# Attention of a hybrid decoder block: where the first tiles' transpositions and products stand among the blocks of scores

## The reference, cut to what matters

```python
def block(args):                       # 128 queries at a time, all heads
    scores = (einsum('bqhd,bkhd->bhqk', qn_b, k_nope)
              + einsum('bqhd,bkd->bhqk', qr_b, k_rope)) * scale
    scores = where(mask, scores, -inf)  # causal
    p = softmax(scores, axis=-1)
    return einsum('bhqk,bkhd->bqhd', p, v)
```

## Time and profile before

| | |
|---|---|
| median of 3 runs | 2707.79 us (2706.94 to 2709.8) |
| the profiled execution: its own time | 2709.62 us |
| the profiled execution: span from first to last instruction | 2707.7 us |
| TensorE busy | 2587.3 us, 96% |
| VectorE busy | 1756.2 us, 65% |
| ScalarE busy | 850.6 us, 31% |
| GpSimd busy | 638.9 us, 24% |
| mean granted TensorE clock | 0.981 of full |
| attention phase, from the first scores to the last product | 1357 to 2160 us |

### The profile page before, as it was taken

One profiled execution on the slowest core, in us unless ns is written; L12 is line 12 of the kernel. 1 busy time (PEld: TensorE's weight loads), 2 busy tenths in 40 slices (PEclk: granted clock), 3 DMA queues, 4 the chain that ended last, 5 costly groups with the idle time before them and its releaser, 6 DMA issues. The chain is left out here.

```text
span 2707.7 us, 32612 instructions
## 1 busy us (share of the span) xinstructions
PE 2587.3 (96%) x12186; PEld 2128.1 (79%) x12186; DVE 1756.2 (65%) x2073; ACT 850.6 (31%) x1683; POOL 638.9 (24%) x592
## 2 busy tenths in 40 slices
PE   4989999999999999997899999999999889999998
PEld 4767888888888888786777887887887778888887
DVE  5787967979879779564367767767767522223442
ACT  3432111111111111232255555555555430201221
POOL 2132111111111111131033233233233220323422
PEclk8999999999999999998899999999999999999999
DMA  8053312212112121377812112112111074666542
GB/s 297 8 175 105 94 32 78 67 58 78 47 55 83 42 78 59 121 263 251 252 63 102 62 65 101 62 65 101 62 65 65 32 240 156 201 216 212 188 151 78
DMA packets 200848, 306.73 MB, mean 113 GB/s; under 512 B 18249, under 2 KB 119693, under 8 KB 190636
## 3 DMA queue, kind: packets, MB, share of 16 engines
q1 hardware_dynamic: 194620, 284.89, 32.1%
q0 software_dynamic: 6128, 20.45, 2.4%
HBM read 202.01 MB, written 103.28 MB: 113 GB/s over the span
## 5 line engine op out<-in xcount | busy, mean ns | idle before, releaser
L52 PE MATMUL ps_proj<-h_hi,w_hi 128*128 128x512 f32 x1696 | 669.5, 395 | 9.6 <-DVE h_lo L697 6.8
L54 PE MATMUL ps_proj<-h_hi,w_lo 128*128 128x512 f32 x1696 | 662.6, 391 | 0.0
L53 PE MATMUL ps_proj<-h_lo,w_hi 128*128 128x512 f32 x1696 | 662.4, 391 | 0.0
L812 DVE SCALAR_TENSOR_TENSOR acc<-u,taps_t,acc 128x2048 f32<-128x2048 f32 x240 | 629.0, 2621 | 8.5
L52 PEld LDWEIGHTS ps_proj<-h_hi,w_hi 128*128 128x128 f32 x1696 | 320.1, 189 | 79.0 <-issue 7.8
L53 PEld LDWEIGHTS ps_proj<-h_lo,w_hi 128*128 128x128 f32 x1696 | 320.1, 189 | 67.5 <-issue 2.2
L54 PEld LDWEIGHTS ps_proj<-h_hi,w_lo 128*128 128x128 f32 x1696 | 319.7, 189 | 67.1
L586 POOL TENSOR_TENSOR w_lo<-raw,w_hi 128x1024 fp32r<-128x1024 f32 x53 | 168.7, 3184 | 807.1 <-ACT w_hi L411 807.0
L1692 POOL TENSOR_SCALAR prob<-prob,rinv 128x512 f32<-128x512 f32 (+2 forms) x320 | 196.3, 630 | 355.3 <-DVE rinv L1646 355.1
L1651 DVE TENSOR_TENSOR pt_lo<-ps_t,pt_hi 128x512 fp32r<-128x512 f32 (+1 forms) x320 | 194.3, 610 | 98.3 <-ACT pt_hi L1574 94.2
L1574 ACT ACTIVATE pt_hi<-ps_t 128x512 fp32r<-128x512 f32 (+1 forms) x320 | 169.4, 531 | 240.7 <-PE ps_t L1486 240.6
(11 more groups left out here) (216 smaller groups left out, 4040.8 us busy)
## 6 DMA issues: line engine op xcount, KB each, us to landing
qlat<-qlat_dram SPq DMA_DIRECT2D x32, 1024.0 KB, 6.1
raw<-in_w_in_dram SPq DMA_DIRECT2D x52, 512.0 KB, 6.4
under_h<-in_w_ada_dram SPq DMA_DIRECT2D x8, 1024.0 KB, 11.2
ga_dram<-lat SPq DMA_DIRECT2D x8, 1024.0 KB, 5.0
gb_dram<-lat SPq DMA_DIRECT2D x8, 1024.0 KB, 5.0
agate_dram<-lat SPq DMA_DIRECT2D x8, 1024.0 KB, 5.0
conv_dram<-acc SPq DMA_DIRECT2D x8, 1024.0 KB, 3.9
bgate_dram<-lat SPq DMA_DIRECT2D x8, 1024.0 KB, 5.0
```

What stands on the lines that cost most here:

```text
L52: pe.matmul(out, wh, xh, start=first, stop=False)
L53: pe.matmul(out, wh, xl, start=False, stop=False)
L54: return pe.matmul(out, wl, xh, start=False, stop=last)
L812: dve.scalar_tensor_tensor(acc[:], u[:, n:n + S], tap(n), acc[:], ALU.mult, ALU.add).then_inc(conv_tap if n < TAPS - 1 else conv_done, 1)
```

## The change

In group 3 the tiles that stand with blocks 5, 6 and 7 now stand behind the first chunk of the block's scores, no longer behind the block. The event `S` of such a block is split into `SA` (first chunk) and `SB` (the other three, and the maximum over the chunks). The event `E` is split as well: `E` is now the exponentials alone, and `R` the reciprocal and the scaling, which stays behind the block's scores. Tile 3 moves from block 7 to block 8 (`share`). The diff:

```diff
@@ attention_phase
     LAG = 2
+    PART = {"S": slice(None), "SA": slice(0, 1), "SB": slice(1, None)}
     SLOTS = 3
@@ plan
-        share = {3: [0, 1, 1, 2], 1: [0, 2, 7, 7], 2: [0, 2, 3, 3]}
+        share = {3: [0, 1, 1, 1], 1: [1, 2, 7, 7], 2: [0, 2, 3, 3]}
         for s, (g, b) in enumerate(BLOCKS):
-            ev.append(("S", s))
+            split = g == NC_ - 1 and b > 0
+            ev.append(("SA" if split else "S", s))
             if s:
                 ev.append(("E", s - 1))
+            if split:
+                tiles(share[g][b])
+                ev.append(("SB", s))
+            if s:
+                ev.append(("R", s - 1))
             if s == 5:
                 ev.append(("W", 0))
             if s in (6, 7):
                 ev.append(("VS", s - 4))
-            if g in share:
+            if g in share and not split:
                 tiles(share[g][b])
-        ev.append(("E", len(BLOCKS) - 1))
+        ev += [("E", len(BLOCKS) - 1), ("R", len(BLOCKS) - 1)]
@@ TensorE
-                def scores(at, s):
+                def scores(at, s, chunks):
...
-                    for c in range(g + 1):
+                    for c in range(g + 1)[chunks]:
...
-                        elif e[0] == "S":
-                            scores(at, e[1])
+                        elif e[0] in PART:
+                            scores(at, e[1], PART[e[0]])
@@ VectorE
-                        elif kind == "S":
+                        elif kind in PART:
                             g, b = BLOCKS[n]
-                            for c in range(g + 1):
+                            for c in range(g + 1)[PART[kind]]:
...
-                            if g:
+                            if g and kind != "SA":
                                 n_max = chunk_no[n, g] + 1 - QB
...
-                        elif kind == "E":
+                        elif kind == "R":
```

## The result

The changed kernel took 2712.4 us (median of 20 runs, 2709.4 to 2718.5), the kernel before 2707.8 us (20 runs): a ratio of 1.0019, interval 1.0013 to 1.0025. So it is slower, by some 5 us (3.5 to 6.8). The direction and the range were right; the forecast of 9.5 us was too high by about a factor of two.

The account below looks back on a forecast made before the run. TensorE, busy 96% of the span, was taken as the bound, with tile 4 following block 7's maximum; 16.92 - 15.73 = 1.19 us, times 8 heads = 9.5 us, on 2707.8 gave 2717.3 us, range 2711.5 to 2721.

Parts of the forecast that it names:

- Tile 4 moves with block 7's maximum: End of block 7: a fixed chain of 5.19 us from its maximum to tile 4, whatever TensorE does in between.
- VectorE's chain of low part, maxima and exponentials: Blocks 4 to 7: maxima queued behind the waiting low part follow the previous exponentials; 1.19 us more per head, chance 0.82.
- T0's gate: Before block 5's second chunk: T0 waits for GpSimd's scaling of block 3, costing 0.5 to 0.8 us of TensorE's time.
- the three transitions: Block 4 to 5, 5 to 6 and 6 to 7: 5.58, 5.70 and 5.64 us, together 16.92 against 15.73 before.
- A wait of about 1 us in front of block 6's second chunk: A sign expected in the trace if right: TensorE waits about 1 us before block 6's second chunk.
- The sign in front of S8's second chunk: A sign expected in the trace if right: a wait of about 0.8 us before the second chunk of block 8's scores.
- The second rival, T0's gate alone: Block 5's second chunk starts late, at 2.2 to 2.5 us; 0.2 to 0.5 us per head, 2709.6 to 2712 us; chance 0.08.
- The first rival, filled waits are won: Blocks 5 to 7: TensorE sets the pace, ring waits are filled; 0.37 us less per head, 2704.8 us; chance 0.06.
- block 5's ring wait of 0.43 us: Between block 5's first and second chunk: 1.67 us where 1.24 would do, so about 0.43 us lost that a transposition could fill.
- a cover of 0.5 us at block 5: Block 5's second chunk is ready at 3.96 us at the latest, VectorE comes to its maximum at 4.42.
- The clock: Blocks 5 to 8: nothing added; as a rival, new waits lower the clock once in each head, 2751 us; chance 0.04.

Follow-up runs that it names:

- e1: The changed kernel with VectorE's low parts of tiles 0 to 2 put back behind the block's maxima and reciprocal; 1.0016 against the kernel before.
- e2: The kernel before with only tile 3 moved from block 7 to block 8; one run, 2707.0 us.
- e5: The changed kernel with block 3's reciprocal and scaling moved between block 4's second and third chunks, so T0 need not wait; 1.0019 against the kernel before.
- e6: The changed kernel with e1's low parts behind the maxima and e5's earlier scaling of block 3 together; 0.9996 against the kernel before.
- e3: The changed kernel with both splits of the values moved behind block 7's exponentials and scaling; 0.9986 against the kernel before.
- e4: The kernel before with both splits of the values moved behind block 7's exponentials and scaling; 0.9984 against the kernel before.
- e8: e6 with the splits of the values behind block 7's exponentials and scaling, and block 7 unsplit with tiles 2 and 3 behind it; 0.9972 against the kernel before.

## Why the prediction was right, and where it was off

*Tile 4 moves with block 7's maximum.* Right. The distance was 5.18 to 5.21 us in before, changed, e1, e2, e5 and e6, whatever TensorE had in between, and it fell only when the split of the values was taken out of GpSimd's list (e3, e4).

*VectorE's chain of low part, maxima and exponentials sets the interval.* Right as the mechanism of the changed kernel for blocks 5 and 6: e5 shows that T0's gate, worth 0.5 us of TensorE's time, is covered by it, as the prediction had it. At block 7 it no longer holds in full. There the prediction had more cover than at block 5, and the trace has none (rows from two narrow windows, the x2 row holding the second and third held maximum):

```profile
1483.14 1.43 DVE L1635 TENSOR_REDUCE nmax<-ps_ring 128x1 f32<-128x512 f32 x2
...
1483.62 0.23 PE L1481 MATMUL ps_ring<-mask,ident 128*128 128x128 bf16 x1
...
1483.88 0.69 DVE L1635 TENSOR_REDUCE nmax<-ps_ring 128x1 f32<-128x512 f32 x1
```

The last maximum starts 0.74 us behind the one before it, not 0.61, and 0.26 us behind its chunk's mask; before the change it was 0.27 (1482.74 to 1483.01). So it waited for TensorE, which had T2 and PV0 in front of these chunks. That is 0.13 of the 16.45 us, read from the trace alone; no run tests it.

*The size of this chain was off.* The term of the sum that was too large is the three transitions, 16.92 us where 16.45 was measured. I had set held maxima one behind the other at their drawn duration of 0.69 us. Standing back to back they start 0.61 us apart (three with a last one of 256 columns take 1.61 us, not 1.77). From the first full maximum to `nbias` block 5 measured 1.65 against 1.81, block 6 1.78 against 1.98, block 7 2.07 (with the 0.13 us of waiting in it) against 2.10: 0.39 us of the 0.47. The rest is the low parts of 384 and 256 columns, 0.47 and 0.34 against my estimates of 0.56 and 0.38, less small differences the other way. The rows had told it: in the earlier trace rows a low part drawn with 0.69 us was followed by a maximum after 0.61. I used the pitch there and the duration in the very next term. As the gain or loss is a difference of two large sums, 3% of one sum was 40% of the difference: 1.19 us forecast, 0.72 measured in the interval, 0.74 in the head.

*A wait of about 1 us in front of block 6's second chunk.* This sign failed: the wait was 0.35 us (1474.61 in the timeline). T0's gate had made TensorE late, so that less was left to wait for; with the gate open (e5) it is 0.63 us. The sign in front of S8's second chunk, about 0.8 us, was right by the prediction's own reckoning: 1485.63 less 1483.65 less 1.24 is 0.74 us.

*The second rival, T0's gate alone, was nearer than its chance of 0.08 said.* Its price of 0.2 to 0.5 us per head is what e1 shows, 0.51. The two limits lie only 0.23 us per head apart. The forecast gave T0's gate a cover of 0.5 us at block 5. It had looked at the second chunk alone, and the cover shrinks from chunk to chunk: TensorE delivers them 1.14 us apart, while held maxima follow each other after 0.61. At block 5's `nbias` only 0.13 us of it are left (5.43 us in the changed kernel, 5.30 in e1; 4.75 in e6, with the gate open as well). In e1 block 7 then takes 5.73 us, as T2 and PV0 stand on the path. Without the held maxima the change would thus still have lost. And the measured time of 2712.4 us lies nearer to this rival's 2712 than to the forecast's 2717.3; that the chain and not the gate is the later limit is shown by e5, not by the time.

*The first rival, filled waits are won.* Its interval was 15.36 us (15.73 less 0.37); e6, in which nothing holds the maxima up and the gate is open, has 15.62, and a head of 101.50 against 101.54. The rival had taken block 5's ring wait of 0.43 us three times over. The kernel before has, from first to second chunk, 1.60 us in block 6 and 1.57 in block 7:

```profile
1472.44 0.48 PE L1466 MATMUL ps_ring<-kn_hi,qn_hi 128*128 128x512 f32 x1
...
1474.04 0.50 PE L1466 MATMUL ps_ring<-kn_hi,qn_hi 128*128 128x512 f32 x1 [0.21 <-ACT prob L1566]
...
1477.64 0.48 PE L1466 MATMUL ps_ring<-kn_hi,qn_hi 128*128 128x512 f32 x1
...
1479.21 0.50 PE L1466 MATMUL ps_ring<-kn_hi,qn_hi 128*128 128x512 f32 x1 [0.17 <-ACT prob L1566]
```

Less the 1.24 us of an unhindered chunk that is 0.36 and 0.33, so 1.12 us in all and not 1.29, and an interval of 15.53. So the thought behind the change is sound for its ring waits, but it is worth next to nothing: block 6 comes 0.30 us sooner behind block 5 (5.15 against 5.45), and T2 and PV0 make block 7 0.18 us later (5.72 against 5.54; in e8, where they stand behind the block again, it is 5.55).

*The clock* stayed at 1.00 in this stretch, and in every 100 us from 1357 to 2057, with waits of up to 0.9 us in each head. The depth-cycling that the Trainium skill tells of (TensorE: Matmul & The Clock Gate, in the section on a second failure mode) did not appear here.

## What to carry to other kernels

Find the last gate of a stage (here GpSimd's scaling in front of tile 4) and ask what a reordering does to the instruction that opens it; the waits that are filled on the way may be free already. Work that is moved forward on one engine moves forward in the in-order lists of all the engines that share the list of events: what is then queued behind its wait on the others (here three maxima behind one low part) has to be counted. Where a forecast is the difference of two chains, take start-to-start distances for every link of both, never durations.

## What was not expected of the hardware

VectorE's drawn durations overlap by 0.08 to 0.09 us when its instructions stand back to back: 0.69 us drawn, 0.60 to 0.61 us from start to start, for full maxima (1482.54 to 1483.14 in the changed kernel) and low parts (1471.34 to 1471.94) alike.
